# Value pages of a paged cache moved from SyncE's DMA queue to GpSimd's, key pages left on SyncE's, in a decoder trunk on one Trainium2 core

## The reference, cut to what matters

```python
k_past = cache_k[page_table].reshape(bs, past_len, SB_HEADS, SB_DH)   # (8, 1024, 12, 64)
v_past = cache_v[page_table].reshape(bs, past_len, SB_HEADS, SB_DH)
...
z = jnp.einsum('bqhd,bkhd->bhqk', q, k).astype(jnp.float32) * (SB_DH ** -0.5)
z = z + bias.astype(jnp.float32)[None, :, None, None]
mask = k_pos[None, :] < q_pos[:, None]
log_keep = jnp.where(mask, jax.nn.log_sigmoid(-z), 0.0)
incl = lax.cumsum(log_keep, axis=3, reverse=True)
excl = jnp.concatenate([incl[..., 1:], jnp.zeros_like(incl[..., :1])], axis=-1)
wts = jnp.where(mask, jnp.exp(jax.nn.log_sigmoid(z) + excl), 0.0)
return jnp.einsum('bhqk,bkhd->bqhd', wts.astype(v.dtype), v)
```

## Time and profile before

| | |
|---|---|
| time, median of 3 runs | 1882.37 us (1876.63 to 1883.95) |
| the profiled execution's own time | 1884.36 us |
| its span, first to last instruction | 1882.5 us |
| TensorE busy | 1763.8 us, 94% |
| VectorE, ScalarE, GpSimd busy | 54%, 38%, 17% |
| page loads | 64 x 256 KB and 64 x 128 KB for keys, as many for values |
| granted TensorE clock, mean | 0.975 of full speed |

### The profile page before, as it was taken

How to read it: one execution, slowest core, us unless ns; L and a number is a source line. 1 busy time by engine, 2 the same in 40 slices (tenths; PEclk the granted TensorE clock), 3 DMA queues, 4 the chain that set the end, 5 groups by cost and what they waited for, 6 DMA issues and landing times. The chain is left out here.

```text
span 1882.5 us, 36354 instructions
## 1 busy us (share of the span) xinstructions
PE 1763.8 (94%) x13404; PEld 1637.5 (87%) x13404; DVE 1013.7 (54%) x1848; ACT 721.2 (38%) x1239; POOL 327.8 (17%) x452
## 2 busy tenths in 40 slices
PE   8999899999799999999999998777899999999997
PEld 6999788887598999999998997444588999999997
DVE  4663455552437667666227333755536676678224
ACT  4343333331545333335226113435446343335222
POOL 1554344452001222221000000000000222221000
PEclk9999999998899999999999999988899999999999
DMA  4222111100521222223231227778721222222322
GB/s 171 78 78 79 70 35 34 33 20 28 174 78 66 81 78 89 78 78 106 89 100 57 79 79 268 224 262 262 246 77 53 84 78 85 82 78 76 101 87 87
DMA packets 90656, 188.62 MB, mean 100 GB/s; under 512 B 9442, under 2 KB 41570, under 8 KB 90194
## 3 DMA queue, kind: packets, MB, share of 16 engines
q1 hardware_dynamic: 90050, 185.26, 29.2%
q0 software_dynamic: 528, 2.32, 0.3%
HBM read 176.00 MB, written 11.55 MB: 100 GB/s over the span
## 5 line engine op out<-in xcount | busy, mean ns | idle before, releaser
L674 PE MATMUL PB<-parts,wparts 128*128 128x288 f32 x8664 | 1169.5, 297 | 22.2 <-DVE wparts L643 11.0
L674 PEld LDWEIGHTS PB<-parts,wparts 128*128 128x128 f32 x8664 | 1163.8, 190 | 26.5 <-DVE wparts L643 21.3
L633 ACT ACTIVATE wparts<-ring 128x1024 fp32r<-128x1024 f32 x198 | 209.9, 1060 | 680.9 <-PE PB L674 680.1
L643 DVE TENSOR_TENSOR wparts<-ring,wparts 128x1024 fp32r<-128x1024 f32 x174 | 213.0, 1225 | 271.3 <-ACT wparts L633 261.7
L1033 POOL COPY cnew<-arena 128x2 f32 (+1 forms) x106 | 113.1, 1067 | 344.8 <-DVE arena L958 342.0
L970 DVE SCALAR_TENSOR_TENSOR arena<-arena,ffw 128x512 f32<-128x512 f32 x176 | 133.2, 757 | 21.1 <-DVE arena L971 12.8
L955 DVE TENSOR_TENSOR arena<-PB,stats 128x288 f32<-128x288 f32 x88 | 40.2, 456 | 126.7 <-PE PB L674 120.1
L684 PE MATMUL PB<-parts,wparts 128*128 128x288 f32 x648 | 104.8, 310 | 3.9 <-DVE parts L513 3.3
L684 PEld LDWEIGHTS PB<-parts,wparts 128*128 128x128 f32 x648 | 91.0, 188 | 12.9 <-DVE parts L513 7.3
L1009 DVE SCALAR_TENSOR_TENSOR arena<-arena,dnw 128x512 f32<-128x512 f32 x54 | 58.0, 1074 | 32.8 <-ACT arena L908 27.6
L932 ACT ACTIVATE arena<-arena,ffw 128x512 f32<-128x512 f32 x88 | 63.9, 726 | 28.9 <-issue 17.1
(11 more groups left out here) (297 smaller groups left out, 2058.0 us busy)
## 6 DMA issues: line engine op xcount, KB each, us to landing
ring<-in_w SPq DMA_DIRECT2D x198, 512.0 KB, 3.2
arena<-in_kpages SPq DMA_DIRECT2D x64, 256.0 KB, 5.2
arena<-in_vpages SPq DMA_DIRECT2D x64, 256.0 KB, 4.8
arena<-in_kpages SPq DMA_DIRECT2D x64, 128.0 KB, 2.2
arena<-in_vpages SPq DMA_DIRECT2D x64, 128.0 KB, 2.3
membuf<-in_w SPq DMA_DIRECT2D x8, 512.0 KB, 5.7
arena<-in_state_dn SPq DMA_DIRECT2D x6, 512.0 KB, 5.0
o_dns_s<-arena SPq DMA_DIRECT2D x6, 512.0 KB, 3.9
```

The costliest lines, as they stand in the source:

```text
L633: nc.scalar.activation(wparts[:, 0, k, :], ring[:, k, :], ACT.Copy).then_inc(hi_ready, 1)
L643: nc.vector.tensor_tensor(wparts[:, 1, k, :], ring[:, k, :], wparts[:, 0, k, :].bitcast(F32), ALU.subtract).then_inc(lo_ready, 1)
L674: last = nc.tensor.matmul(dst(b), wparts[:, part, k, block * P:(block + 1) * P], x[:, row_, b * HALF:(b + 1) * HALF], start=start and part ...
```

## The change

`page_number`, `keep_pages` and `page_loads` move into a function `page_loader(eng)`, which gives each engine its own kept numbers. SyncE calls it for the key granules and skips the value granules; GpSimd calls it for the value granules in a new `pool_values`, which stands right behind `pool_queries`. Every number is now kept: `keep_pages` takes two pairs of sequences at a time and reads only those that it doesn't hold. Keys and values get separate landing semaphores, since the two queues now fill the same slots.

```diff
-        page_in, page_used = [sem(f"page_in{i}") for i in range(SLOTS)], sem("page_used")
+        page_in = {kind: [sem(f"{kind}page_in{i}") for i in range(SLOTS)] for kind in "kv"}
+        page_used = sem("page_used")
...
-            return 16 * sum(gran_pages[n % SLOTS:n + 1:SLOTS])
+            return 16 * sum(gran_pages[m] for m in range(n % SLOTS, n + 1, SLOTS) if grans[m][0] == grans[n][0])
...
+        def page_loader(eng):
+            page_at = {}
+            def page_number(at):
+                return eng.value_load(pages[0:1, at:at + 1])
+            def keep_pages(*pairs):
+                for at in [a for a in page_at if a // (2 * PAGES) not in pairs]:
+                    del page_at[at]
+                for pair in pairs:
+                    for at in range(2 * pair * PAGES, 2 * (pair + 1) * PAGES):
+                        if at not in page_at:
+                            page_at[at] = page_number(at)
+            def page_loads(n):
...
+                if n >= SLOTS:
+                    eng.wait_ge(page_used, n - SLOTS + 1)
+                for x in range(gran_pages[n]):
+                    at = (2 * (pair + x // 4) + bb) * PAGES + 4 * span + x % 4
+                    eng.dma_start(to[:, x, :], cache[bass.ds(page_at[at], 1), :, f0 * P:f0 * P + wide].rearrange(
+                        "a p n -> p (a n)")).then_inc(page_in[kind][n % SLOTS], 16)
+            return keep_pages, page_loads
+
+        def pool_values(pool):
+            keep_pages, page_loads = page_loader(pool)
+            for n, (kind, k, bb, span) in enumerate(grans):
+                if kind == "v":
+                    if (bb, span) == (0, 0) and k in (0, 2, 3):
+                        keep_pages(*{0: (0, 1), 2: (1, 2), 3: (2, 3)}[k])
+                    page_loads(n)
...
                     pool_queries(pool)
+                    pool_values(pool)
...
-            keep_pages(0)
+            keep_pages, page_loads = page_loader(sp)
+            keep_pages(0, 1)
             for n in range(3):
                 page_loads(n)
             sp.wait_ge(m_mixed, nth(1, NCH))
             for n in range(3, len(grans)):
                 kind, k, bb, span = grans[n]
-                if kind == "k" and k > 1 and k != 4 and (bb, span) == (0, 0):
-                    keep_pages(block_of(k, 0)[0])
-                page_loads(n)
+                if kind == "k":
+                    if (bb, span) == (0, 0) and k in (3, 4):
+                        keep_pages(*{3: (1, 2), 4: (2, 3)}[k])
+                    page_loads(n)
```

More of the change, by code:

```diff
@@ L1905, in pe_set_z @@
                     n = gran_no["k", k, bb, span]
-                    pe.wait_ge(page_in[n % SLOTS], landed(n))
+                    pe.wait_ge(page_in["k"][n % SLOTS], landed(n))
                     for g in range(4):
@@ L1949, in pe_set_a @@
                 n = gran_no["v", k, bb, span]
-                pe.wait_ge(page_in[n % SLOTS], landed(n))
+                pe.wait_ge(page_in["v"][n % SLOTS], landed(n))
                 for c in range(4):
@@ L2196, in dve_sb @@
                     dve_set_c(dve, p + 1)
+        def page_loader(eng):
[10 more added lines that the diff above has]
+            def page_loads(n):
+                kind, k, bb, span = grans[n]
+                cache = d[f"{kind}pages"]
+                pair, f0 = block_of(k, 0)
+                wide = 256 if k % 3 == 1 else 512
+                to = slot(n).rearrange("p (c n) -> p c n", n=wide)
+                if n >= SLOTS:
[12 more added lines that the diff above has]
+                    page_loads(n)
         def pool_queries(pool):
@@ L2533, in _ @@
             feed("v")
[L2535 to L2559, removed]
             feed("in_b")
```

## The result

The changed kernel takes 1886.2 us, median of 20 runs (1877.71 to 1890.4), beside 1882.32 us for the kernel before, also of 20 runs: a ratio of 1.0022, 95% interval 1.0011 to 1.0032. The forecast was 1877 us. The profiled execution has a span of 1884.2 us.

The account below looks back on a forecast made before the run. The prediction took the cache-streaming stage to be bound by SyncE's issue. Page waits falling from 28.7 to 23.7 us (-5.0) gave 1884.4 - 5.0 = 1879.4, 1877 us against the median; its own range 1871 to 1884, with rivals 1860 to 1896.

Parts of the forecast that it names:

- The bound: Stage streaming the sample cache: bound by SyncE's issue of all 256 page loads, which reaches TensorE as 28.7 us of waits.
- the sum of waits behind the second queue: TensorE's page waits with values on GpSimd's queue: 3.5 + 3 x 3.9 + 5.7 + 2.8 = 23.7 us instead of 28.7.
- pairs 1 and 4: Head pairs with 128 KB value loads: wait 5.7 us beside keys in pair 1, 2.8 us by GpSimd's issue in pair 4.
- c: Third, last but one, value granule of a pair; its issue needs a slot that the burst's key matmuls free; wanted at z+8.2.
- d: Last value granule of a pair, wanted at z+9.3; forecast to land at z+13.2 in pairs 0, 2 and 3.
- rival A: VectorE's two 0.82 us minimum operations per pair hold GpSimd's issue: c and d 1.6 us later, +8.0 us, 1885 us; chance 0.25.
- z: Start of a burst's key matmuls on TensorE, from which each pair's times are counted; slots forecast free from z+0.9.
- Sharing in pairs 0 and 2: Next set's keys and late values share the DMA engines evenly: a 3.9 us wait in pairs 0, 2 and 3.
- The start: TensorE's wait at its first key matmuls: 2.7 us becomes 3.5, an estimate (2.7 to 7.4), from 16 more SyncE reads ahead.
- The clock: Granted clock halves after long waits, some 2 us per pair: no change forecast, from -8 to +2 since pair 0 joins.
- Rival B: GpSimd a poor issuer in every pair: 0.8 us an issue, 4.0 us to landing, waits 37.8 us, 1893 us; chance 0.20.
- Rival C: Keys do not slow values: no wait in pairs 0, 2, 3, waits 9.1 us in all, 1859 us; chance 0.15.

Follow-up runs that it names:

- the minimum in other form: Changed kernel with VectorE's two minimum operations per pair written with two tensor operands (duration 0.82 to 1.48 us): 1885.6 us, ratio 1.0016 to before.
- the keys held for d: Changed kernel, but SyncE starts the key pages of set k+2 only when the last value page of set k has landed: 1873.4 us, ratio 0.9954 to before.
- the swapped kernel: Against the changed kernel, values go on SyncE's queue and keys from set 2 on through GpSimd's: 1893.2 us, ratio 1.0055 to before.

## Why the prediction was wrong, step by step

- **The bound** (SyncE's issue) was right: fewer reads alone give 6 us, and after the change SyncE waits for slots. What I did not do is price the two parts apart. That 1877 is what kept numbers alone measure is chance: the forecast was for both parts, and the second queue costs 0.58% on top.
- **The step that failed is the sum of waits behind the second queue:** 23.7 us forecast, 30.5 measured. With 28.7 before, the waits grew by 1.8 us where I had them fall by 5.0. Two terms carry it: the held issue, which the sum put at nothing (3.2 us), and pairs 1 and 4, mis-sized by 3.5 us. c is waited for in all five pairs, where the forecast had one wait, before d. The hold alone is not the answer: without it 27.2 us of waits are left, 1.5 below before and not 5.0, and the time, 1885.6, can't be told from 1886.2.
- **The held issue.** The sum took GpSimd's issue as free of VectorE, with rival A outside it at 0.25. The hold is there in all five bursts. A's size was off too: 8.0 us put down, 3.2 us of waits measured, in pairs 0, 2 and 3 alone. The issue starts at z+1.74 and not at z+0.9, so it meets only the rest of the two operations and is 0.87 us longer, not 1.6. That A's time, 1885, came out nearly right is luck, since taking the hold away leaves the time there. The Trainium skill, SBUF — State Buffer, "A bandwidth-pool intuition that's wrong (but worth ruling out)", says that a load through GpSimd's queue beside a VectorE copy is blocked until about 115 ns after the copy's end. For the minimum operations here the trace agrees, with 0.12 us.
- **Sharing in pairs 0 and 2** came out to a tenth: 3.9 us forecast, and 3.90 and 3.89 us where the hold is taken away. Part of that is luck, for two errors cancel: there GpSimd's first issue comes 0.85 us later than taken (z+1.74), and the shares are not even. The keys move from z+4.7 on, about when forecast (z+4.6), but in the 8 us after that the values (q0) take more than half (pair 0 of the changed kernel with the minimum in other form, 1218.2 to 1226.2):

```profile
q0 software_dynamic: 508, 1.63, 54.6%
q1 hardware_dynamic: 608, 1.12, 41.5%
```

  Pair 3 has 4.8 us. What I missed there is that the sharing could be avoided, for 12.8 us, by one wait on SyncE.
- **Pairs 1 and 4** were mis-sized: 5.7 and 2.8 us forecast, 7.7 and 4.3 measured, and the same without the hold. In pair 4 (z = 1338.35) no keys run, so it is GpSimd's issue: it starts 0.85 us later than taken, and its sixteenth load is issued at z+11.03, not z+9.15. It lands 2.6 us after its issue, not 3.0:

```profile
1349.38 0.55 POOL L2226 DMA_DIRECT2D arena<-in_vpages  x1 [0.15 <-issue]
1351.99 1.93 PE L1954 MATMUL PB<-arena,membuf 128*32 128x128 f32 x32 [2.42 <-DMA arena<-in_vpages]
```

  In pair 1 (z = 1240.39) the sixteenth issue comes at the same point, z+10.95, but d's matmuls begin at z+17.9, 4.3 us later than in pair 4. So there it is the bytes, and the shares are uneven the other way. From z+4 to z+10 the keys (q1, 256 KB a load) move nearly twice as much as the values (q0, 128 KB):

```profile
q1 hardware_dynamic: 668, 1.23, 56.9%
q0 software_dynamic: 242, 0.66, 40.2%
```

- **The start** cost 2.8 us instead of 3.5. Waits add up: 23.7 - 0.7 + 3.2 + 0.9 + 3.5 = 30.6, beside 30.5 measured; 1877 + 6.8 is 1884. The last 2 us lie in the step from one execution to the medians. The forecast took 2.0 us off because the profiled execution of before lay above its median; that of after (1885.85 us) does not. From profile to profile the time grows by 1.5 us, for 1.8 us of waits; the medians differ by 3.9 us (2.1 to 6.0).
- **The clock**, put at no change, went the way of its upper end: the first pair joined, but for 1.1 us (24.95 to 26.03 us of TensorE work), not 2.
- **Rival B** was wrong in its price: with the keys held, value loads of 128 KB land in 3.5 us (median), not 4 and more. **Rival C** is refuted by the 1.93 and 1.75 MB above. The Trainium skill, DMA: Bandwidth & Descriptors, "Issuing engines are not separate DMA queues", says that loads of all issuers interleave on the same engines, and that a second issuer only saves issue time. The trace agrees with the first (51.0% and 47.0%). The second is too kind here: with numbers kept, the second queue costs 0.58%, since it also lets a later load in beside an urgent one.

## What to carry to other kernels

One queue does two things: it limits issue, and it keeps prefetch behind what is wanted now. If a stage is issue-bound, first make each issue cheaper: the kept numbers alone (0.9964) can't be told from two queues with the keys held for d (0.9954), since their intervals overlap. Then try a second issuer for the same transfer; where two streams go to two queues, let the prefetch wait for the landing of the urgent one. Before moving loads to GpSimd's queue, look for VectorE's operations at the moment of the issue and for register reads between the issues.

## What the runs showed of the hardware that I had not expected

- A read of a page number on GpSimd just ahead of a load adds 0.34 us to the spacing (0.58 to 0.92 us); the 32 reads made in advance are over by 1166.7, before TensorE's first key matmuls free a slot.
- GpSimd's first load starts some 0.85 us after the slot is free by the forecast's count (z+1.74, z+0.9); SyncE's key loads start 0.3 us after theirs (z+3.0, z+2.7).
- An issue beside VectorE's minimum operations ends 0.12 us after one of them: in the changed kernel's five bursts after the second of a back-to-back pair, with each operation done twice after every one of the four, also where no gap follows.
- Two queues do not share the engines in fixed halves. With 256 KB a load on both, GpSimd's moved 1.63 MB beside 1.12 MB of SyncE's in 8 us, and 1.93 beside 1.75 MB from 1213.4 to 1223.7 in the changed kernel. Beside loads of 128 KB, those of 256 KB moved more on either queue: 1.23 MB on SyncE's beside 0.66, and 4.20 MB on GpSimd's beside 3.10 in the swapped kernel.
